# A decoder-layer kernel: 256 tokens instead of 192 take their expert sums from fetched rows, and four of 16 sum tiles stay in PSUM

## The reference

```
def block(xb):                         # xb: 128 tokens x 1024
    qh = (xb @ peer_w_query)...        # 8 heads, two half queries each
    v1, i1 = lax.top_k(s1, 16); v2, i2 = lax.top_k(s2, 16)
    vals, flat = lax.top_k(cand, 16)   # 16 of 16384 experts, for each of 8 heads
    e = i1[...] * 128 + i2[...]
    g = jax.nn.softmax(vals, axis=-1)
    act = jax.nn.gelu(jnp.einsum('thkd,td->thk', peer_u[e], xb))
    return jnp.einsum('thk,thkd->td', g * act, peer_v[e])
```

## Time and profile before

| what | value |
|---|---|
| median of 3 runs | 5143.03 us (5133.89 to 5150.5) |
| the profiled execution: its time, its span | 5135.67 us, 5134.0 us |
| PE / DVE / ACT / POOL busy over the span | 93% / 56% / 26% / 14% |
| granted TensorE clock, mean over the span | 0.921 |
| dots phase, first to last dot product | 2335.6 to about 3866 us |
| sums phase, first to last matmul | 3896.9 to 5067.5 us |

### The profile page before, as it was taken

The page is one execution under the profiler, slowest core; times in us unless marked ns, Lnnn a source line. Parts: engine busy times, 40 slices in busy tenths (PEclk is TensorE's granted clock), DMA queues, the critical chain, the costliest instruction groups (busy, mean ns, idle before and its releaser), DMA issues. The chain is left out here.

```text
span 5134.0 us, 70840 instructions
## 1 busy us (share of the span) xinstructions
PE 4780.4 (93%) x26838; PEld 2997.6 (58%) x26838; DVE 2899.9 (56%) x5280; ACT 1342.2 (26%) x1843; POOL 711.8 (14%) x617
## 2 busy tenths in 40 slices
PE   5999989989778798999999999999997999999996
PEld 4666643368676465666666666666663555555553
DVE  3466325521355435215666676667536888888884
ACT  2223124410110001112444444444322222212120
POOL 0000000011000000000000000000004555544620
PEclk6999988965676899999999999999998999999998
DMA  4443410043233444214555555565538777777751
GB/s 150 161 155 138 155 33 19 14 146 107 88 114 101 152 160 153 85 59 149 182 186 182 205 182 183 183 210 175 176 122 285 247 249 260 239 258 251 254 191 70
DMA packets 364749, 825.07 MB, mean 161 GB/s; under 512 B 32946, under 2 KB 203570, under 8 KB 355442
## 3 DMA queue, kind: packets, MB, share of 16 engines
q1 hardware_dynamic: 259314, 480.84, 27.9%
q0 software_dynamic: 61376, 243.41, 13.6%
q10 hardware_dynamic: 43840, 97.93, 5.1%
HBM read 639.85 MB, written 182.22 MB: 160 GB/s over the span
## 5 line engine op out<-in xcount | busy, mean ns | idle before, releaser
L365 PE MATMUL dot_ps<-h_parts,u_parts 128*128 128x384 f16 (+1 forms) x9216 | 1455.6, 317 | 7.9 <-PEq L1795 4.8
L365 PE MATMUL totals_ps<-act_parts,v_parts 128*128 128x448 f16 x6144 | 1166.2, 353 | 37.4 <-DVE act_parts L2651 35.1
L365 PEld LDWEIGHTS dot_ps<-h_parts,u_parts 128*128 128x128 f16 x9216 | 891.0, 98 | 498.0 <-issue 8.0
L365 PEld LDWEIGHTS totals_ps<-act_parts,v_parts 128*128 128x128 f16 x6144 | 600.6, 98 | 601.9 <-issue 38.5
L378 PE MATMUL in_ps<-h_parts_in,in_parts 128*128 128x384 f16 (+1 forms) x3168 | 492.2, 318 | 5.4 <-DVE in_parts L694 4.5
L2385 DVE SCALAR_TENSOR_TENSOR u_parts<-u_chunks,units,u_parts 128x1024 f16<-128x1024 f32 x126 | 161.8, 1284 | 508.2 <-ACT u_parts L2170 508.1
L2660 DVE SCALAR_TENSOR_TENSOR h<-totals_ps,sum_unit,h 128x448 f32<-128x448 f32 x512 | 335.7, 679 | 173.5 <-PE totals_ps L365 173.0
L2179 ACT ACTIVATE gelu<-dot_ps,units 128x384 f32<-128x384 f32 (+1 forms) x384 | 215.9, 563 | 802.3 <-PE dot_ps L365 802.2
L378 PEld LDWEIGHTS in_ps<-h_parts_in,in_parts 128*128 128x128 f16 x3168 | 308.8, 98 | 182.9 <-DVE in_parts L694 4.6
L2611 ACT ACTIVATE v_parts<-v_group,units 128x1024 f16<-128x1024 f32 x128 | 136.5, 1137 | 838.8 <-PE totals_ps L365 811.1
L2716 POOL DMA_INDIRECT row_value<-tmp_g_rows,row_g x192 | 291.9, 1520 | 308.1 <-POOLq L2045 249.8
(11 more groups left out here) (339 smaller groups left out, 5372.0 us busy)
## 6 DMA issues: line engine op xcount, KB each, us to landing
u_chunks<-in_u SPq DMA_DIRECT2D x128, 512.0 KB, 5.6
v_sweep<-in_v SPq DMA_DIRECT2D x128, 512.0 KB, 4.8
v_group<-in_v SPq DMA_DIRECT2D x32, 2048.0 KB, 8.5
tmp_g<-gelu ACTq DMA_DIRECT2D x128, 448.0 KB, 2.7
tmp_w<-h POOLq DMA_DIRECT2D x28, 2048.0 KB, 8.2
w_groups<-tmp_w SPq DMA_DIRECT2D x32, 1792.0 KB, 11.5
gelu_in<-tmp_g SPq DMA_DIRECT2D x32, 1792.0 KB, 8.3
merge_sweep<-in_u POOLq DMA_DIRECT2D x64, 512.0 KB, 5.6
```

Of the source, the lines that this page charges most:

```text
L365: mm = pe.matmul(bank, left(x), right(y), start=first and x == 0 and y == 0, stop=last and x == 1)
```

## The change

TD falls from 896 to 832. The 64 tokens 832 to 895 join the rows, so that two full tiles of 128 tokens go by rows: NROWS is 256. Tile 6 is now half dense: 16 of its 32 `weights` blocks and 4 of its 8 `onehots` go, and `keep_rows` runs for it also. Each of the 6144 matmuls of the sums has 416 columns instead of 448. Every fourth of the 16 output tiles is **held**: it has a PSUM bank of its own (banks 4 to 7), accumulates through all 32 groups, and DVE adds it once, in the last group. The other 12 share 4 banks. The ring of rows has 5 buffers. A group has 8 or 9 rows (6 or 7 before), from chunk m = 0 on. The turning back of the row sums at the end is 4 lots of 4 transposes in place of 2 such lots and one of 8 small matmuls.

```
-TD = (TILES - 1) * P
+TD = (TILES - 1) * P - TS
-NROWS = FULL + FULL // 2
+NROWS = 2 * FULL
...
+        def tokens_of(t):
+
+            return TD - PART * P if isinstance(t, int) and t == PART else P
...
                         for n in due(x, q):
-                            weights(t, n)
+                            if n * 4 < tokens_of(t):
+                                weights(t, n)
...
-                    if dense and x in ONEHOT_AT:
+                    if dense and x in ONEHOT_AT and ONEHOT_AT[x] * SUB < tokens_of(t):
                         onehots(t, ONEHOT_AT[x])
                     if not dense and x == 0:
-                        keep_rows(t)
+                        keep_rows(t, 0, ((0, P, 0, FULL, 0),))
+                    if tokens_of(t) < P and x == 3:
+                        keep_rows(t, 1, ((tokens_of(t), P, 0, FULL, FULL),))
...
-        RR, BATCH = 4, 8
+        RR, BATCH = 5, 8
...
-        BANKS = 4
-        ps = ctx.enter_context(nc.psum_tensor("totals_ps", [P, BANKS, 512], F32))
-        back_ps = ctx.enter_context(nc.psum_tensor("row_sums_ps", [P, 512], F32))
+        BANKS, HELD = 4, 4
+        ps = ctx.enter_context(nc.psum_tensor("totals_ps", [P, BANKS + HELD, 512], F32))
+        back_ps = ps[:, BANKS, :]
...
+        def held(at):
+
+            return at % EVERY == EVERY - 1
+
+        def bank(at):
+
+            return BANKS + at // EVERY if held(at) else (at - at // EVERY) % BANKS
...
-                            pe.wait_ge(sum_taken, g * PER + at + 1)
+                            if not held(at):
+                                pe.wait_ge(sum_taken, g * MOVED + at - at // EVERY + 1)
+                            begins = not held(at) or isinstance(g, int) and g == 0
+                            ends = not held(at) or isinstance(g, int) and g == LAST
                             for j in range(GRP):
-                                mm = triple(pe, ps[:, at % BANKS, 0:n],
+                                mm = triple(pe, ps[:, bank(at), 0:n],
...
                         at = m * ND + q
+                        if held(at) and g < LAST:
+                            continue
                         dve.wait_ge(sum_done, (g + 1) * PER + at + 1)
...
                         for at, x in enumerate(rows):
-                            if KC - len(rows) + at == m:
+                            if at * KC // len(rows) == m:
                                 add_row(x)
```

More of the change, by code:

```diff
@@ L145, in constants @@
     c[:, C_PAIR:C_PAIR + TS] = p[:, None] % TS == np.arange(TS)[None, :]
-    c[:, C_TOK], c[:, C_TOK + 1] = p, P + p % TS
+    c[:, C_TOK], c[:, C_TOK + 1] = TS + p, np.where(p < TS, TS + P + p, p - TS)
     return c
@@ L2031, in dots_phase @@
         ONEHOT_AT = {1: 0, 2: 1, 4: 2, 5: 3, 7: 4, 8: 5, 10: 6, 11: 7}
-        DENSE = TD // P
+        DENSE = TILES - 1
+        PART = DENSE - 1
+        def tokens_of(t):
+            return TD - PART * P if isinstance(t, int) and t == PART else P
         def rounds(eng, body):
@@ L2402, in _, with keep_rows @@
                 dve.sem_inc(right_ready, 1)
-                def keep_rows(t):
+                def keep_rows(t, first, parts):
                     dve.wait_ge(picked, t + 1)
-                    small = t - DENSE
                     one, two = spot[:, 0, :], spot[:, 1, :]
@@ L2417, in keep_rows @@
                     link.link(dve.tensor_scalar(place_f[:, :], place_f[:, :], float(ROW_W),
[L2418 to L2421, removed]
+                                                const[:, C_TOK + first:C_TOK + first + 1], ALU.mult, ALU.add))
+                    for p0, p1, c0, c1, to in parts:
                         for dst, src in ((s["row_v"], spot[:, 2, :]), (s["row_g"], place_f[:, :]),
@@ L2462, in _ @@
                     if x == 0:
-                        keep_rows(TILES)
+                        keep_rows(TILES, 1, ((0, TS, 0, FULL, FULL),))
                     if x < TAIL // 2:
@@ L2503, in sums_phase @@
         coef_ready, row_added = sem("row_coef_ready"), sem("row_added")
-        back_done, back_taken = sem("back_done"), sem("back_taken")
+        back_done, back_taken, held_taken = sem("back_done"), sem("back_taken"), sem("held_taken")
         w_in = [sem(f"wt_in{r}") for r in range(2)]
@@ L2512, in sums_phase @@
         PER = KC * ND
+        EVERY = PER // HELD
+        MOVED = PER - HELD
         NBATCH = NROWS // BATCH
         WORKED = NGRP - 2
-        big = s["h"][:, :, TD:SEQ]
+        big = [s["h"][:, :, t * P:(t + 1) * P] for t in range(TILES - 1, TILES)]
+        FULLS = len(big) * FULL
+        BACKS = len(big) * 2 + 2
         LAST = NGRP - 1
@@ L2520, in flat, with rounds @@
             return x.rearrange("p (b t) -> p b t", t=TB)
-        def rounds(eng, turn):
-            with eng.Fori(0, LOOPS) as i:
+        def held(at):
+            return at % EVERY == EVERY - 1
+        def bank(at):
+            return BANKS + at // EVERY if held(at) else (at - at // EVERY) % BANKS
+        def rounds(eng, turn, first=0):
+            for r in range(2 * first):
+                turn(r, r % 2, r // 2)
+            with eng.Fori(first, LOOPS) as i:
                 for r in range(2):
@@ L2568, in back @@
                 def back(b):
-                    pe.wait_ge(row_added, 1 + (FULL if b < 2 else NROWS))
+                    pe.wait_ge(row_added, 1 + (FULL * (b // 2 + 1) if b < 2 * len(big) else NROWS))
                     if b > 0:
                         pe.wait_ge(back_taken, b)
+                    else:
+                        pe.wait_ge(held_taken, 1)
                     const = s["const"]
[L2574 to L2581, removed]
+                    for n in range(4):
+                        k = b % 2 * 4 + n
+                        src = big[0][:, k, :] if b < 2 else sums[:, k * P:(k + 1) * P]
+                        mm = pe.transpose(back_ps[:, n * P:(n + 1) * P], src, const[:, C_ID:C_ID + P])
                     mm.then_inc(back_done, 1)
@@ L2589, in total @@
                             at = m * ND + q
-                            pe.wait_ge(sum_taken, g * PER + at + 1)
+                            if not held(at):
+                                pe.wait_ge(sum_taken, g * MOVED + at - at // EVERY + 1)
+                            begins = not held(at) or isinstance(g, int) and g == 0
+                            ends = not held(at) or isinstance(g, int) and g == LAST
                             for j in range(GRP):
-                                mm = triple(pe, ps[:, at % BANKS, 0:n],
+                                mm = triple(pe, ps[:, bank(at), 0:n],
                                             lambda x: v16[:, r, x, j, m * P:(m + 1) * P],
-                                            lambda y: a16[:, r, y, j, t0:t0 + n], j == 0, j == GRP - 1)
+                                            lambda y: a16[:, r, y, j, t0:t0 + n], begins and j == 0,
+                                            ends and j == GRP - 1)
                             mm.then_inc(sum_done, 1)
-                        if isinstance(g, int) and g == LAST and m in (2, 4, 6):
-                            back(m // 2 - 1)
+                        if isinstance(g, int) and g == LAST and 2 <= m < 2 + BACKS:
+                            back(m - 2)
                 pe.sem_inc(sum_done, PER)
-                rounds(pe, total)
+                rounds(pe, total, 1)
             @block.scalar
@@ L2623, in _ @@
                 rounds(act, turn)
-                for b in range(3):
+                for b in range(BACKS):
                     act.wait_ge(back_done, b + 1)
-                    x = back_ps[:, :].rearrange("p (k t) -> p k t", t=P if b < 2 else TS)
-                    to = big[:, b * 4:(b + 1) * 4, :] if b < 2 else s["h"][:, :, SEQ:T]
-                    act.copy(to, x).then_inc(back_taken, 1)
+                    x = back_ps.rearrange("p (k t) -> p k t", t=P)
+                    k = slice(b % 2 * 4, (b % 2 + 1) * 4)
+                    if b < 2:
+                        act.copy(big[0][:, k, :], x).then_inc(back_taken, 1)
+                    else:
+                        act.copy(s["h"][:, k, SEQ:T], x[:, :, 0:TS])
+                        act.copy(s["h"][:, k, TD:TD + TS], x[:, :, TS:P]).then_inc(back_taken, 1)
             @block.vector
@@ L2657, in add @@
                         at = m * ND + q
+                        if held(at) and g < LAST:
+                            continue
                         dve.wait_ge(sum_done, (g + 1) * PER + at + 1)
                         x = acc[:, m, t0:t0 + n]
-                        dve.scalar_tensor_tensor(x, ps[:, at % BANKS, 0:n], sum_unit[:, :], x, ALU.mult,
-                                                 ALU.add).then_inc(sum_taken, 1)
+                        dve.scalar_tensor_tensor(x, ps[:, bank(at), 0:n], sum_unit[:, :], x, ALU.mult,
+                                                 ALU.add).then_inc(held_taken if held(at) else sum_taken, 1)
```

(2 more changed lines are left out.)

## The result

The changed kernel takes 5099.0 us (median of 7, 5075.6 to 5115.5) against 5139.5 (7 runs, 5133.9 to 5150.5): ratio 0.9926, 95% interval 0.9905 to 0.9948, 40 us less. The profiled execution took 5107.65 us, span 5106.0, 28 less than before. The runs lie within 40 us of each other, those of before within 17.

A forecast was written before the change was run, and what follows sets the result against it. It took POOL's fetch loop as the new bound, with PE setting the pace before: -7.3 - 82.0 + 61 = -28 us, 5107 from the profiled execution or 5115 from the median; forecast 5112 us, range 5046 to 5165.

The forecast's parts named there:

- B: POOL's queue: time to issue the 8 values ahead of a batch of rows, between 14.9 and 19.9 us, taken as 17.4.
- PE's bound: Sums: 6144 matmuls of 416 columns save 82.0 us; PE then needs 33.75 us a group instead of 36.3.
- the loop: POOL's fetches with a ring of 5: 16.2 + B, 33.6 us against PE's 31.6, in 31 batches +61 us; chance 0.5.
- the first rival: Sums: PE keeps the pace as B is at most 15.4 us; time 5046, chance 0.2.
- The dots phase: Dots phase on PE: 16 blocks of 8 weight matmuls go, 0.46 us each, -7.3 us.
- Slack of 11 us: Sums: PE has some 11 us of slack between two freed banks, so single DVE stalls are forgiven and mean pace decides.
- DVE's wait: Sums: DVE's waiting for PE would be nearly gone, from 173 us.
- PE keeping the pace: The first rival: in the sums B is at most 15.4 us, time 5046, chance 0.2.
- The slower kernel: Rival on POOL's fetches: B is 19.9 us in every batch, +138 us, time 5184; chance 0.18.
- Slower transfers: Rival on the DMA engines: 86% share instead of 73%; 1 us more from issue to use gives 5138; chance 0.12.
- the term of 5.9 us from issue to use: Part of the loop: the first row of the next batch, from its issue to its use, 5.9 us.
- the prediction's own price of 31 us for each microsecond: Fetches: if a row's issue to use grows by 1 us, the kernel takes 31 us more.

The follow-up runs named there:

- the mended ones: The changed kernel with a ring of 6 row buffers, 5042.4 us, or with its POOL queue in another order, 5046.6 us; both together 5041.3 us.
- the interleaved kernel: The changed kernel with POOL issuing the value of row n + 8, then row n, instead of 8 values then 8 rows: 5046.6 us, ratio 0.9818.

## Why the prediction was right

Forecast 5112 us, measured 5099.0, by the mechanism that was forecast. That the sum comes so near is in part luck, as the point on B shows.

- **PE's bound.** With the loop closed (ring of 6) the sums took from 3882.3 to 4966.2 us, 1083.9, 33.9 a group; predicted 33.75. Kernels with the loop closed take 5041 to 5047 us; the first rival's time was 5046. Before, the sums took from 3896.9 to 5067.2, 1170.3, so the shorter matmuls saved 86 us and not 82. The changed kernel's took 3891.7 to 5039.4, and its loss is 1147.7 - 1083.9 = 64 us against the 61 of the prediction.
- **The dots phase** went from 1525.9 us (first to last dot product, which starts at 3861.5 and not at about 3866 as in the table of before) to 1520.1, and is 1519 to 1521 in four of the experiments: -6, not -7.3. Between the phases 2 us were saved that I had put at nothing.
- **The loop** is the cause: leaving out its values, adding a buffer, or changing only the order of the queue each ends the wait, and none of them touches DVE's work or the rows. The timelines show it batch by batch, with B from the issue of the first value to that of the row behind the last. The loop closes up to B = 31.6 - 16.2 = 15.4 us with a ring of 5, and by the same count, 3.5 us of DVE's row interval less or more, up to 11.9 with 4 and 18.9 with 6. In the changed kernel 14 of 30 batches are longer than 15.4, and DVE stood still for 4.1 to 11.0 us behind each. With the ring of 4 all 30 are too long (12.6 to 20.7) and DVE stood still behind each. With the ring of 6 none is (10.2 to 17.7), and PE waited 0.4 us in all.
- **B was the middle of too narrow a pair, and one B for all batches was the wrong step.** The mean is 8 x (1.647 + 0.30) = 15.6 us, below my 17.4, and the long batch is 23.6, above my 19.9. With that mean in each of 31 batches the prediction's loop gives 31 x 0.2 = 6 us. Stalls do not come in each batch, but in some 20 waits of up to 11 us; what the 14 long batches are too long by adds up to 45 us, where the sums phase lost 64; with the ring of 4 it adds up to 116, where it lost 123. The middle value stood in for the spread, and that is the luck in the sum. Stalls in only a part of the batches may also be why the runs spread by 40 us, where those of the ring of 4, with a stall in each batch, lie within 9 and those of the ring of 6 within 15; this was not tested.
- **Slack of 11 us, and DVE's wait.** "Single stalls of DVE are forgiven" held in part: 121 us of DVE's stalls cost PE 47, but the stall of 11.0 us shown above cost it 8.5, since DVE was already behind: PE went on for only 4.4 us after DVE had stopped (4037.2 to 4041.6). DVE's wait for PE, to be nearly gone, is still 65 us, but 41 of them come after 4960 us, when the rows are done, and 18.5 from 4620 to 4800, where no batch was long.
- **A term I left out is the clock.** The windows of the changed kernel hold 5674 matmuls in 1060 us; with the ring of 6 there are 1025 in each 180 us, so those need 996 us. Of the 64 us lost, PE stood still for 47 and lost the other 17 at a lower clock. Behind the stall of 8.5 us shown above, busy time by stage has it:

```profile
4050.00:4060.00 10.00, 9.88 (x43) 4.83 (x43) 10.00 (x13) 3.21 (x4) 7.49 (x4) 0.74 0.65 206
4060.00:4080.00 20.00, 20.00 (x115) 11.15 (x114) 19.00 (x22) 0.64 (x1) 16.33 (x13) 1.00 0.72 257
```

 PE works almost without a pause, but at a mean of 0.74 of 2.4 GHz, and does 43 matmuls in 10 us where it later does 57. From 4036 to 4041 us, before the stall, the granted clock was 1.00; from 4050 to 4053 it was 0.50, the level of 1.2 GHz; from 4056 on it was 1.00 again. So PE's idle time came out under the forecast of 60 and the whole at it.
- **The rivals.** PE keeping the pace: false for this kernel, true for each of the mended ones. The slower kernel: false. The ring of 4 does make a slower one, but at the same cost of a value, 1.65 us, so by the ring and not by a B of 19.9 in every batch. Slower transfers: the ring of 6 and the interleaved kernel run at 81 to 90% share of the DMA engines up to 4800 us with next to no wait, so the share is not the cause by itself. But the term of 5.9 us from issue to use came from one batch. It is 8.0 in the batch above, and the median from issue to landing went from 7.1 to 7.7 us (`rows_in`) and from 5.9 to 7.8 (`rstd`). By the prediction's own price of 31 us for each microsecond, that is a part of the loss; how large a part, and what lengthened it, no run shows.
- **The Trainium skill,** page "SBUF — State Buffer", section "Who interferes with whom", has the rule that a DVE instruction with two SBUF inputs contends with a GpSimd instruction that reads SBUF; by that rule, the run with row sums in PSUM agrees (issues under a row add: mean 2.11 us with the sum in SBUF, none above 0.96 with it in PSUM). Its remark that a `tensor_tensor` was not seen to stall a DMA's issue differs from the 1.74 us of the earlier trace rows; the measurement decides.

Not settled: why an issue that waits gets in between two such DVE instructions in some places and not in others (4.40 us above is a row add and two of `rest_v` without a gap). No run here takes that apart.

## What to carry to other kernels

When work is moved from a dense engine to fetched rows, cost the fetch as a loop: from the freeing of a buffer through everything queued ahead of the next issue to its use, against the pace of the bounding engine. Cost it with the long blocks too and not with the mean alone, which here gave 6 us of the 64. Side transfers belong between the rows, not in a block ahead of them, and a ring is to be suspected when its rows last less than that block and one row's issue to use together; here either mend sufficed without moving any work. An engine at 89% is not the bound by its share, but it can slow the engine that feeds it. The changed kernel and the one without held tiles, which lost most to stalls in only a part of their batches, spread by 40 and 47 us between runs, all others by 26 or less; such a spread is a reason to look for a loop of this kind.

## What the runs showed of the hardware that was not expected

The issue of an indirect transfer on POOL took 0.94 us, with 0.30 between two, beside an idle DVE or one with a large input in PSUM, and up to 4.41 beside DVE instructions with two inputs in SBUF. An accumulating DVE instruction costs the same with its running sum in PSUM as in SBUF (1280 and 1278 ns for 1024 elements). After a stall of PE of 8.5 us the granted clock was 0.50 for 3 us and was back at 1.00 some 6 us after PE's start; over the first 10 us its mean was 0.74.
